# First three weight panels of each layer: own buffers, converted in the stage in front, the third panel in two token halves

## The chip, the cores and the metric

The kernel runs on one core of a Trainium2 chip. The metric is the device time of one execution in microseconds (us), and lower is better. Engines are named as in the profile: PE is TensorE (PEld its weight loads), ACT is ScalarE, DVE is VectorE, POOL is GpSimd, SP is SyncE, which issues the DMAs.

## What is computed

One sequence of 512 tokens with 1024 features (float32) goes through one block of a first kind and two layers of a second kind. The first block is a token mixer (convolution and an RWKV recurrence), then a feed-forward part (FFN):

```python
h = h + _rms_norm(mix, post_mix_g[l])
ffn = _channel_mixer(_rms_norm(h, pre_ffn_g[l]), ...)   # w_up 1024x5632, conv, gelu*up, w_down 2816x1024
h = h + _rms_norm(ffn, post_ffn_g[l])
```

Each layer of the second kind, run twice, is:

```python
h = _rms(x, norm_g[l])
proj = h @ w_in[l]
... = jnp.split(proj, SPLIT_AT, axis=-1)      # gq gk gv ga gz bq bk bv iq ik iw bz cq ck cv cz gate
y_a, y_b, y_c = gated linear attention, top-k attention, differential attention
merged = g0 * (y_a @ w_br[l, 0]) + g1 * (y_b @ w_br[l, 1]) + g2 * (y_c @ w_br[l, 2])
x = x + merged @ w_out[l]
```

## The kernel before

Five engines run five instruction streams written out by hand; semaphores that count each engine's finished steps order them. There are four stages: `mixer`, `ffn`, `layer` 0 and `layer` 1 (in `program`).

**Split products.** Every large product is made of three matmuls on float32r parts: weight hi x h hi, weight hi x h lo, weight lo x h hi (`project`, PE line L596). The weights come in panels, mostly 1024 rows x 256 columns, held as 128 x 2048. A panel goes through four steps. SP loads it into `m.raw` ("w raw"), ACT copies it to `m.wh` (`split_hi`, L352), DVE subtracts to get `m.wl` (`split_lo`, L393), and PE uses both ("w used"). `split_hi_halves` and `split_lo_halves` (L364, L374) do the two steps in halves. The three tensors have two slots each, taken in turn by the panel's running number `g`. So SP loads panel p when "w lo" of p-2 is done, and ACT converts it when PE has used p-2.

**The entry of a layer.** The stage in front ends with partial sums for blocks of 128 tokens. In the FFN these are the last two down panels, kk = 9 and 10 (`down`, L2036), in the order (9,0), (9,1), (10,0), (10,1), (9,2), (9,3), (10,2), transposes of blocks 0 and 1, (10,3). In layer 0 they are the last two `out` panels in a like order. Between the stages lies a seam. For each block of tokens: ACT sums squares (`post_sum`, `pre_sum`: L418, L421), DVE scales and adds (`post_add`: L466, L470, L474; `half_add`: L482) and norms (`pre_norm`: L490, L496, the result is xn), PE transposes (`seam_turn`, L586), ACT copies to h_hi (`seam_hi`, L447), DVE makes h_lo (`seam_lo`, L457). Blocks 0 and 1 come first, then 2 and 3.

The layer's first panels are iq[0] (256 columns), `lows` (ik, ga and iw together, 88 columns, three DMAs) and iq[1] (256 columns), then gk. In `tensor`, iq[0] and lows run first for tokens 0 to 255 (half 0), then for tokens 256 to 511 (half 1) with the transposes of blocks 2 and 3 between; iq[1] runs after both, over all 512 tokens. In `scalar` and `vector` the conversions of panels 0 and 1 (`high(0)`, `high(1)`, `low(0)`, `low(1)`) stand between the steps of the seam, the halves of panel 2 behind them.

**SP's order.** In the FFN the load of down panel kk waits for "w lo" of kk-2. Then come the layer's panels 0 and 1, each behind "w lo" of two panels before, then `rows_in` (14 small DMAs: 8 rows of norm gains, 4 lambda vectors, 2 of the gate projection), then panel 2 and the rest.

**ACT and DVE at the FFN's end.** For kk from 2 to 10 ACT does w_hi of down panel kk (not for 10), then the copy ffn_hi of kk (L2095), which waits for PE to have used kk-2; after the loop w_hi of panel 10 in halves. DVE does ffn_lo (L2142), then w_lo, and at the end w_lo of panel 10 in halves.

Of the kernel before, what the change touches and what calls it, by code (L numbers as in the profile page):

```python
# [12 lines left out]
F32 = mybir.dt.float32  # L13
# [5 lines left out]
P = 128  # L19
# [1925 lines left out]
def ffn(m, A, done, sems, seam, after, base):  # L1945
# [119 lines left out]
    def scalar(E):  # L2065
# [23 lines left out]
        for kk in range(2, DN):  # L2089
            if kk < DN - 1:  # L2090
                split_hi(E, m, down_base + kk, PANEL)
            E.wait_ge(act_done, E.so_far())
            E.wait_ge(dve_done, E.at(("G", 2 * kk + 1)))
            E.wait_ge(pe_done, E.at(("dn mm", kk - 2)))
            act.activation(m.gH[:, kk % 2, :, :], m.G[:, 2 * kk:2 * kk + 2, :], ACT.Copy).then_inc(act_done, 1)  # L2095
            E.counted(("g hi", kk))
        split_hi_halves(E, m, down_base + DN - 1, PANEL)
        seam_table(E, m, after)

    def vector(E):  # L2100
# [67 lines left out]
def lay_out_layers(nc, m):  # L2168
# [50 lines left out]
    m.wa2 = take("gla_wa2", [LOWS + LOWS // 3, 256])  # L2219
    m.later = m.bd  # L2220
    at[0], end = m.fcol_at, at[0]
    m.lcol = take("layer_cols", [P, 16])
# [10 lines left out]
def layer(m, A, out, done, sems, l, base, seam, after):  # L2233

    pe_done, act_done, dve_done, pool_done = (done[n] for n in ("pe", "act", "dve", "pool"))
    PS = m.PS
    w_loaded = sems("w_loaded0"), sems("w_loaded1")
    rows_loaded, small_loaded, gain_loaded, stored = (sems(n) for n in ("rows_loaded", "small_loaded", "gain_loaded", "stored"))

# [39 lines left out]
    def view(buf, p):  # L2279
        a = panels[p]  # L2280
        return buf[:, (base + p) % 2, 0:a.kt * a.w].rearrange("p (k n) -> p k n", k=a.kt)

    def size(p):
        return panels[p].kt * panels[p].w
# [51 lines left out]
    def sync(E):  # L2336
# [21 lines left out]
        for p in range(NP):  # L2358
            E.wait_ge(*E.point(("w lo", base + p - 2)))
            v, at, n = view(m.raw, p), 0, 0  # L2360
            pieces, kt, k0 = panels[p].pieces, panels[p].kt, panels[p].k0
            ks = kt if len(pieces) > 1 else kt // 2
            for name, c, w in pieces:
                for k in range(0, kt, ks):
                    if name in (0, 1, 2):
                        s = A["w_br_2"][l, name, P * k:P * (k + ks), c:c + w]
                    else:
                        s = A[name][l, P * (k0 + k):P * (k0 + k + ks), c:c + w]
                    sp.dma_start(v[:, k:k + ks, at:at + w],
                                 s.rearrange("(k q) n -> q k n", q=P)).then_inc(w_loaded[(base + p) % 2], 16)  # L2370
                    n += 1
                at += w
            E.moved(("w raw", base + p), f"w_loaded{(base + p) % 2}", n)
            if p == 1:
# [32 lines left out]
    def tensor(E, banks):  # L2407
# [7 lines left out]
        def panel(p, only=None, half=None):  # L2415
            a = panels[p]
            E.wait_ge(*E.point(("w lo", base + p)))
            H, W = view(m.wh, p), view(m.wl, p)
            ts = slice(0, T) if half is None else slice(PW * half, PW * half + PW)
# [25 lines left out]
        def tokens_part(p, t, k):  # L2445
            a = panels[p]
            H, W = view(m.wh, p), view(m.wl, p)
# [88 lines left out]
        for half in range(2):  # L2536
            for q in range(2):
                E.wait_ge(dve_done, E.at(seam.key("lo", 2 * half + q, 1)))
            if half:
                panel(iq[0], half=1)  # L2540
                panel(lows, half=1)
            elif seam.post is None:
                panel(iq[0], only=0, half=0)
                seam_turn(E, m, banks, seam, 2)
                panel(iq[0], only=1, half=0)
                seam_turn(E, m, banks, seam, 3)
                panel(lows, half=0)
            else:
# [3 lines left out]
                seam_turn(E, m, banks, seam, 3)  # L2552
        panel(iq[1])
        E.wait_ge(*E.point("rows"))
# [156 lines left out]
    def scalar(E):  # L2711
        act = E.eng

        def high(p):
            if p < NP:
                split_hi(E, m, base + p, size(p))

# [125 lines left out]
        if seam.post is not None:  # L2843
            for t in range(2):
                post_sum(E, m, seam, t)
            for t in range(2):
                pre_sum(E, m, seam, t)
            high(0)
# [4 lines left out]
            high(1)  # L2853
        else:
            pre_sum(E, m, seam, 0)
            pre_sum(E, m, seam, 1)
            seam_hi(E, m, seam, 0)
            high(0)
            seam_hi(E, m, seam, 1)
        for t in range(2, TT):  # L2860
            pre_sum(E, m, seam, t)
        if seam.post is None:
            high(1)
# [150 lines left out]
        merged_hi(KT - 1)  # L3014
        high(outs[2])
        high(outs[3])
        if after:
            seam_table(E, m, after)

    def vector(E):  # L3020
# [152 lines left out]
        if seam.post is not None:  # L3173
            for t in range(2):
                post_add(E, m, seam, t)
            for t in range(2):
                pre_norm(E, m, seam, t)
            low(0)
            seam_lo(E, m, seam, 0)
            seam_lo(E, m, seam, 1)  # L3180
            for t in range(2, TT):
                post_add(E, m, seam, t)
            low(1)
        else:
# [3 lines left out]
            seam_lo(E, m, seam, 0)  # L3188
            low(0)
# [5 lines left out]
        if seam.post is None:  # L3195
            low(1)
# [196 lines left out]
        low(outs[1])  # L3393
        low(outs[2])
        low(outs[3])
        for t in order(outs[1]):
# [99 lines left out]
```

## Time and profile before

| what | value |
|---|---|
| runs | 1939.05, 1939.12, 1939.25 us; median 1939.12 |
| profiled execution, its own time | 1943.69 us |
| its span in the trace | 1942.0 us, 30355 instructions |
| mean granted clock of PE | 0.995 |
| PE, PEld, DVE, ACT, POOL busy | 98%, 79%, 60%, 39%, 2% |
| entry of layer 0, entry of layer 1 | about 715 to 770, about 1322 to 1372 us |

The profile is of one execution, and times in its rows count from the start of its span. A row of the timeline has the start, the busy time, the engine, the line of the kernel, what is written and read, and in brackets how long the engine stood before it and who released it. A matmul's end is modelled, and successive matmuls overlap, so their rate is read from their starts.

### The profile page before, as it was taken

What the parts mean: (1) busy time and instruction counts of PE and PEld (TensorE: products, weight loads), DVE (VectorE), ACT (ScalarE), POOL (GpSimd) and SP (SyncE); (2) the same over time, 40 slices, a digit from 0 to 9 for tenths busy, and PEclk for the clock granted to TensorE, in tenths of its full rate; (3) what the DMA queues carried; (4) which work ended last, traced back from release to release, by engine and by line L of the source; (5) the groups of instructions that cost most, each with busy time, mean ns of one, the idle gap of its engine ahead of it and who ended that gap; (6) DMA issues with size and microseconds to landing.
All of it is one profiled execution on the core that took longest, in us unless ns stands there. A gap on an engine that the chain in (4) does not pass through costs nothing.

```text
span 1942.0 us, 30355 instructions
## 1 busy us (share of the span) xinstructions
PE 1901.2 (98%) x12689; PEld 1538.2 (79%) x12689; DVE 1158.0 (60%) x1714; ACT 749.6 (39%) x1082; POOL 32.1 (2%) x72
## 2 busy tenths in 40 slices
PE   7999999999999999999999999999999999999999
PEld 5677778888888888787777788888787777778887
DVE  5854554677675344456687855545446678764534
ACT  5623333422222344533444434334533445334421
POOL 3000000020000000000000000000000000000000
PEclk9999999999999999999999999999999999999999
DMA  4311113233333323222123222232322222222232
GB/s 151 95 55 46 36 35 114 62 109 92 104 88 107 109 76 109 65 88 83 48 71 104 87 66 76 76 130 66 100 75 78 85 66 76 87 87 66 66 109 87
DMA packets 166021, 161.65 MB, mean 83 GB/s; under 512 B 13877, under 2 KB 150363, under 8 KB 165883
## 3 DMA queue, kind: packets, MB, share of 16 engines
q1 hardware_dynamic: 165184, 158.99, 26.0%
q8 instruction: 99, 1.62, 0.4%
q10 hardware_dynamic: 698, 0.71, 0.1%
q14 instruction: 40, 0.32, 0.1%
HBM read 157.59 MB, written 2.10 MB: 82 GB/s over the span
## 4 chain that ended last, share of the span: by engine, by line
PE 77%; DVE 2%; ACT 1%; issue 0%; ACTq 0%; DVEq 0%
PE psum L596 63%; PE psum L2036 5%; PE psum L2531 2%; PE psum L2508 1%; PE psum L586 1%; PE psum L2488 1%; PE psum L2516 1%; DVE w_lo L393 1%; PE psum L523 1%; ACT w_hi L352 0%; PE psum L532 0%; PE psum L2612 0%; DVE h_lo L457 0%; DVE ffn_normed L470 0%; PE psum L2597 0%; DVE w_lo L374 0%
## 5 line engine op out<-in xcount | busy, mean ns | idle before, releaser
L596 PE MATMUL psum<-h_hi,w_hi 128*128 128x512 f32 (+1 forms) x1568 | 611.7, 390 | 10.7 <-DVE h_lo L457 6.1
L596 PE MATMUL psum<-h_lo,w_hi 128*128 128x512 f32 (+1 forms) x1568 | 595.5, 380 | 0.0
L596 PE MATMUL psum<-h_hi,w_lo 128*128 128x512 f32 (+1 forms) x1568 | 595.4, 380 | 0.0
L393 DVE TENSOR_TENSOR w_lo<-w_raw,w_hi 128x2048 fp32r<-128x2048 f32 (+2 forms) x143 | 299.4, 2094 | 284.1 <-ACT w_hi L352 281.6
L352 ACT ACTIVATE w_hi<-w_raw 128x2048 fp32r<-128x2048 f32 (+1 forms) x148 | 260.8, 1762 | 369.8 <-PE psum L596 299.1
L596 PEld LDWEIGHTS psum<-h_hi,w_hi 128*128 128x128 f32 x1568 | 295.3, 188 | 88.1 <-issue 15.7
L596 PEld LDWEIGHTS psum<-h_hi,w_lo 128*128 128x128 f32 x1568 | 295.5, 188 | 56.3
L596 PEld LDWEIGHTS psum<-h_lo,w_hi 128*128 128x128 f32 x1568 | 295.7, 189 | 51.9 <-issue 0.2
L596 PE MATMUL psum<-w_hi,h_hi 128*128 128x512 f32 (+1 forms) x512 | 183.9, 359 | 2.6 <-DVE w_lo L393 1.7
L596 PE MATMUL psum<-w_lo,h_hi 128*128 128x512 f32 (+1 forms) x512 | 179.8, 351 | 0.0
L596 PE MATMUL psum<-w_hi,h_lo 128*128 128x512 f32 (+1 forms) x512 | 179.7, 351 | 0.0
L596 PEld LDWEIGHTS psum<-w_hi,h_hi 128*128 128x128 f32 x512 | 97.6, 191 | 30.0 <-issue 11.0
L596 PEld LDWEIGHTS psum<-w_hi,h_lo 128*128 128x128 f32 x512 | 97.7, 191 | 12.9
L596 PEld LDWEIGHTS psum<-w_lo,h_hi 128*128 128x128 f32 x512 | 97.7, 191 | 11.9 <-issue 0.2
L596 PE MATMUL psum<-y_hi,w_hi 128*128 128x512 f32 x192 | 80.1, 417 | 0.0
L596 PE MATMUL psum<-y_hi,w_lo 128*128 128x512 f32 x192 | 75.2, 392 | 0.0
L596 PE MATMUL psum<-y_lo,w_hi 128*128 128x512 f32 x192 | 75.1, 391 | 0.0
L2126 DVE TENSOR_SCALAR ffn_conv<-psum,ffn_cols 128x512 f32<-128x512 f32 x44 | 35.6, 810 | 63.3 <-PE psum L596 62.2
L2814 ACT ACTIVATE squares<-psum 128x512 f32<-128x512 f32 x48 | 28.7, 598 | 110.6 <-PE psum L596 110.2
L2036 PE MATMUL psum<-w_hi,ffn_hi 128*128 128x512 f32 x176 | 68.7, 390 | 0.5 <-DVE ffn_conv L2132 0.5
L2036 PE MATMUL psum<-w_lo,ffn_hi 128*128 128x512 f32 x176 | 68.5, 389 | 0.0
L2036 PE MATMUL psum<-w_hi,ffn_lo 128*128 128x512 f32 x176 | 68.5, 389 | 0.0
(370 smaller groups left out, 2185.5 us busy)
## 6 DMA issues: line engine op xcount, KB each, us to landing
w_raw<-in_w_in_dram SPq DMA_DIRECT2D x170, 512.0 KB, 4.4
w_raw<-in_w_up_dram SPq DMA_DIRECT2D x44, 512.0 KB, 5.1
w_raw<-in_w_out_dram SPq DMA_DIRECT2D x24, 512.0 KB, 4.5
w_raw<-in_w_br_dram SPq DMA_DIRECT2D x48, 256.0 KB, 3.0
w_raw<-in_w_down_dram SPq DMA_DIRECT2D x22, 512.0 KB, 4.3
x_first<-in_x_dram SPq DMA_DIRECT2D x4, 512.0 KB, 5.1
x_tokens<-in_x_dram SPq DMA_DIRECT2D x4, 512.0 KB, 5.1
out_dram<-x_tokens SPq DMA_DIRECT2D x4, 512.0 KB, 2.6
```

What stands on the lines that cost most here:

```text
L352: act.eng.activation(m.wh[:, g % 2, 0:n], m.raw[:, g % 2, 0:n], ACT.Copy).then_inc(act.done, 1)
L393: eng.eng.tensor_tensor(m.wl[:, g % 2, 0:n], m.raw[:, g % 2, 0:n], m.wh[:, g % 2, 0:n].bitcast(F32), ALU.subtract).then_inc(eng.done, 1)
L523: last = pe.eng.matmul(out[q, :], m.ind[:, kind, q], x[:, j, :], start=begin, stop=end, skip_group_check=True)
L586: last = pe.eng.transpose(m.PS[0:n, bank, rows * i:rows * i + rows], b, m.ident[at:at + rows, at:at + rows])
L596: last = pe.eng.matmul(out, a(k), b(k), start=(opens and k == 0 and i == 0), stop=(k == kt - 1 and i == 2), skip_group_check=ks is not None)
L2036: last = pe.matmul(PS[:, 2 * t + n, :], g[:, kk % 2, k, tt], w[:, k, cc], start=(kk == 0 and k == 0 and i == 0), stop=(kk == DN - 1 and k ...
L2126: dve.tensor_scalar(c, z, tap[2], bias, ALU.mult, ALU.add).then_inc(dve_done, 1)
L2488: pe.matmul(o[:, 0:vis], m.Q[r, h // 2, P * i:P * i + P], m.ikf[r, 0:vis], start=True, stop=True).then_inc(pe_done, 1)
L2508: last = pe.matmul(o[:, 0:vis], m.Q[r, h, P * i:P * i + P], m.K[r, h, 0:vis], start=True, stop=True)
L2516: pe.matmul(o[:, 0:vis], m.Q[:, h, P * i:P * i + P], m.K[:, h, 0:vis], start=True, stop=True).then_inc(pe_done, 1)
L2531: last = pe.matmul(o[:, 0:P], m.V[:, k, P * h:P * h + P], m.PT[:, u % 2, P * k:P * k + P], start=(k == 0), stop=(k == i))
L2814: act.activation(m.sq3[:, 2 * (r % 2) + i, :], PS[:, bank(p, i), :], ACT.Tanh, scale=0.5).then_inc(act_done, 1)
```

## The change

Panels 0, 1 and 2 of each layer no longer use the two slots. Each has its own raw and hi buffer, laid over parts of the layers' arena that are free at that time; its lo is written over its raw. SP loads them without a wait for a slot: for layer 0 after the FFN's last "G", for layer 1 after "dsa lo" of layer 0. Their order to the other DMAs stays, `rows_in` between panels 1 and 2. Panels 3 and 4 take the slots behind the last two panels of the stage in front (`slot_user`).

In the FFN, ACT converts panels 0, 2, 1 after ffn_hi of kk = 9, and DVE subtracts in the same order after w_lo of kk = 9. In layer 0, ACT converts panels 0 and 1 between w_hi of the third and of the fourth `out` panel and panel 2 after the fourth; DVE subtracts 0 and 1 before the w_lo of the fourth, and panel 2 inside the seam, after h_lo of block 0. The conversions in the entries go. ACT's `high(3)` and DVE's `low(3)` follow the seam, `high(4)` and `low(4)` come where `step(iq[1])` had them or sooner.

iq[1] runs in two token halves, its first behind the transposes of blocks 2 and 3, its second last, and uses PSUM banks 3 and 5 instead of 0 and 1.

```diff
+def spare_hi(act, first, g, i):
+    raw, hi, _ = first[i]
+    act.wait_ge(*act.point(("w raw", g + i)))
+    act.wait_ge(act.done, act.so_far())
+    act.eng.activation(hi[:, :], raw[:, :], ACT.Copy).then_inc(act.done, 1)
+    act.counted(("w hi", g + i))
+
+def spare_lo(dve, first, g, i):
+    raw, hi, lo = first[i]
+    dve.wait_ge(dve.done, dve.so_far())
+    dve.wait_ge(dve.sems["act"], dve.at(("w hi", g + i)))
+    dve.eng.tensor_tensor(lo[:, :], raw[:, :], hi[:, :].bitcast(F32), ALU.subtract).then_inc(dve.done, 1)
+    dve.counted(("w lo", g + i))
@@ ffn, scalar: after "g hi" of kk
+            if kk == DN - 2:
+                E.wait_ge(dve_done, E.at(("g lo", 7)))
+                for i in (0, 2, 1):
+                    spare_hi(E, m.first, down_base + DN, i)
@@ ffn, vector: after w_lo of kk
+            if kk == DN - 2:
+                for i in (0, 2, 1):
+                    spare_lo(E, m.first, down_base + DN, i)
@@ lay_out_layers
+    spare = o - 4 * KB + 3 * 4 * PANEL
+    m.first = []
+    for i, n, lo_at, hi_at in ((0, PANEL, o - 4 * KB, q + 8 * KB), (1, KT * LOWP, spare, spare + 4 * KT * LOWP),
+                               (2, PANEL, o - 4 * KB + 8 * PANEL, o - 4 * KB + 4 * PANEL)):
+        m.first.append((take(f"first_raw{i}", [P, n], F32, over=lo_at), take(f"spare_hi{i}", [P, n], F32R, over=hi_at),
+                        take(f"spare_lo{i}", [P, n], F32R, over=lo_at)))
@@ layer
+    def slot_user(p):
+        return base + p - {3: 4, 4: 6}.get(p, 2)
@@ layer, bank
+        if p == iq[1]:
+            return 3 + 2 * i
@@ layer, sync
         for p in range(NP):
-            E.wait_ge(*E.point(("w lo", base + p - 2)))
+            if p == 0 and l == 0:
+                E.wait_ge(dve_done, E.before(None, ("G", FT - 1)))
+            if p == 0 and l:
+                E.wait_ge(dve_done, E.before(l - 1, ("dsa lo", NH - 1)))
+            if p >= 3:
+                E.wait_ge(*E.point(("w lo", slot_user(p))))
@@ layer, tensor
             if half:
                 panel(iq[0], half=1)
                 panel(lows, half=1)
+                panel(iq[1], half=1)
             elif seam.post is None:
                 panel(iq[0], only=0, half=0)
                 seam_turn(E, m, banks, seam, 2)
                 panel(iq[0], only=1, half=0)
+                panel(lows, half=0)
                 seam_turn(E, m, banks, seam, 3)
-                panel(lows, half=0)
+                panel(iq[1], half=0)
             else:
                 panel(iq[0], half=0)
                 panel(lows, half=0)
                 seam_turn(E, m, banks, seam, 2)
                 seam_turn(E, m, banks, seam, 3)
-        panel(iq[1])
+                panel(iq[1], half=0)
@@ layer, scalar: entry (high(0) and high(1) go from both branches)
         seam_hi(E, m, seam, 2)
         seam_hi(E, m, seam, 3)
+        high(3)
         evac(iq[0], 0)
-        split_hi_halves(E, m, base + 2, size(2))
         evac(iq[0], 1)
+        high(4)
         evac(lows, 0)
-        high(3)
-        step(iq[1])
+        evac(iq[1], 0)
+        evac(iq[1], 1)
@@ layer, scalar: end
         high(outs[2])
+        if after:
+            spare_hi(E, m.first, base + NP, 0)
+            spare_hi(E, m.first, base + NP, 1)
         high(outs[3])
         if after:
+            spare_hi(E, m.first, base + NP, 2)
             seam_table(E, m, after)
@@ layer, vector: entry (low(0) and low(1) go from both branches)
             seam_lo(E, m, seam, 0)
-            low(0)
+            spare_lo(E, m.first, base, 2)
             half_add(E, m, seam, 2)
...
-        split_lo_halves(E, m, base + 2, size(2))
         low(3)
-        step(iq[1])
+        low(4)
@@ layer, vector: end
         low(outs[2])
+        if after:
+            spare_lo(E, m.first, base + NP, 0)
+            spare_lo(E, m.first, base + NP, 1)
         low(outs[3])
```

## Rows read from the trace of the kernel before

**Rows 1.** The page: busy time, share of the span and instructions

```profile
PE 1901.2 (98%) x12689; PEld 1538.2 (79%) x12689; DVE 1158.0 (60%) x1714; ACT 749.6 (39%) x1082; POOL 32.1 (2%) x72
```

**Rows 2.** Waits of PE, 693 to 772 (waited for: us, times, longest)

```profile
PE psum L596 <- DVE h_lo L457: 3.2, 2, 2.5
PE psum L596 <- DVE w_lo L374: 1.0, 1, 1.0
PE psum L596 <- DVE w_lo L393: 0.4, 1, 0.4
```

**Rows 3.** Timeline of PE, 1337 to 1359: start, us, engine, line, operation [idle before <-releaser]

```profile
1338.31 0.36 PE L596 MATMUL psum<-h_hi,w_hi 128*128 128x256 f32 x1 [0.42 <-DVE h_lo L457]
...
1358.39 0.50 PE L596 MATMUL psum<-h_hi,w_hi 128*128 128x512 f32 x1 [0.98 <-DVE w_lo L374]
```

**Rows 4.** Timeline of PE, 731 to 746

```profile
731.57 0.28 PE L596 MATMUL psum<-h_lo,w_hi 128*128 128x256 f32 x1
...
737.08 0.28 PE L596 MATMUL psum<-h_hi,w_lo 128*128 128x256 f32 x1
...
745.07 0.36 PE L596 MATMUL psum<-h_hi,w_hi 128*128 128x256 f32 x1 [2.50 <-DVE h_lo L457]
```

**Rows 5.** Windows of PE: length, busy (x), granted clock, DMA share, GB/s

```profile
746.34:749.72 3.38, 3.38 (x18) 0.50 0.00 0
364.00:371.00 7.00, 5.13 (x30) 0.76 0.47 129
375.00:380.00 5.00, 2.50 (x22) 1.00 0.01 3
```

**Rows 6.** Timeline of DVE, 700 to 740

```profile
708.41 1.23 DVE L2142 TENSOR_TENSOR ffn_lo<-ffn_hidden,ffn_hi 128x1024 fp32r<-128x1024 f32 x1 [5.38 <-ACT ffn_hi L2095]
...
709.67 2.48 DVE L374 TENSOR_TENSOR w_lo<-w_raw,w_hi 128x1024 fp32r<-128x1024 f32 x2
...
726.03 2.29 DVE L393 TENSOR_TENSOR w_lo<-w_raw,w_hi 128x2048 fp32r<-128x2048 f32 x1 [0.52 <-ACT w_hi L352]
...
734.24 1.28 DVE L470 SCALAR_TENSOR_TENSOR ffn_normed<-psum,row_stats,post_ffn_gain 128x1024 f32<-128x1024 f32 x1
...
736.82 0.89 DVE L393 TENSOR_TENSOR w_lo<-w_raw,w_hi 128x704 fp32r<-128x704 f32 x1
...
737.94 1.28 DVE L496 SCALAR_TENSOR_TENSOR x_tile<-x_tokens,row_stats,layer_gain 128x1024 f32<-128x1024 f32 x1
```

**Rows 7.** Timeline of ACT, 705 to 735

```profile
707.25 1.06 ACT L2095 ACTIVATE ffn_hi<-ffn_hidden 128x1024 fp32r<-128x1024 f32 x1 [7.87 <-PE psum L2036]
...
708.40 2.16 ACT L364 ACTIVATE w_hi<-w_raw 128x1024 fp32r<-128x1024 f32 x2
...
732.32 0.79 ACT L352 ACTIVATE w_hi<-w_raw 128x704 fp32r<-128x704 f32 x1
```

**Rows 8.** Chain that ended last, 705 to 775: start, us, what

```profile
756.33 11.20 PE psum L596 x48
```

**Rows 9.** Timeline of DVE, 1325 to 1340

```profile
1333.70 2.29 DVE L393 TENSOR_TENSOR w_lo<-w_raw,w_hi 128x2048 fp32r<-128x2048 f32 x1 [2.04 <-ACT w_hi L352]
```

**Rows 10.** Timeline of ACT, 1300 to 1320

```profile
1314.45 1.92 ACT L352 ACTIVATE w_hi<-w_raw 128x2048 fp32r<-128x2048 f32 x1 [8.96 <-PE psum L596]
```

**Rows 11.** Timeline of SP's DMA queue, 690 to 720

```profile
692.18 0.80 SPq L1976 DMA_DIRECT2D w_raw<-in_w_down_dram  x2
...
703.06 10.96 SPq L2369 DMA_DIRECT2D w_raw<-in_w_in_dram  x5
...
719.26 0.28 SPq L2355 DMA_DIRECT2D gla_wa<-in_gla_ba_dram  x1
```

**Rows 12.** DMA issues, 690 to 710 and 1300 to 1330: count, KB, us to landing

```profile
w_raw<-in_w_in_dram SPq DMA_DIRECT2D x2, 512.0 KB, 4.1
...
layer_gain<-in_norm_g_dram SPq DMA_DIRECT2D x1, 512.0 KB, 6.7
```

**Rows 13.** Timeline of PE at the last down panel

```profile
712.41 0.40 PE L2036 MATMUL psum<-w_hi,ffn_hi 128*128 128x512 f32 x1
```

More of the change, by code:

```diff
@@ L2161 @@
 LOWS = RANK + IH
+LOWP = 64 + LOWS
 TAU = 16.0
@@ L2220, in lay_out_layers @@
     m.later = m.bd
+    spare = o - 4 * KB + 3 * 4 * PANEL
[4 more added lines that the diff above has]
+                        take(f"spare_lo{i}", [P, n], F32R, over=lo_at)))
+    assert spare + 8 * KT * LOWP <= pt + 2 * KB
     at[0], end = m.fcol_at, at[0]
@@ L2237, in layer @@
     w_loaded = sems("w_loaded0"), sems("w_loaded1")
+    first_loaded = [sems(f"first_loaded{i}") for i in range(3)]
     rows_loaded, small_loaded, gain_loaded, stored = (sems(n) for n in ("rows_loaded", "small_loaded", "gain_loaded", "stored"))
@@ L2281, in view, with hi_view, lo_view @@
         return buf[:, (base + p) % 2, 0:a.kt * a.w].rearrange("p (k n) -> p k n", k=a.kt)
+    def hi_view(p):
+        return m.first[p][1][:, :].rearrange("p (k n) -> p k n", k=KT) if p < 3 else view(m.wh, p)
+    def lo_view(p):
+        return m.first[p][2][:, :].rearrange("p (k n) -> p k n", k=KT) if p < 3 else view(m.wl, p)
+    def slot_user(p):
+        return base + p - {3: 4, 4: 6}.get(p, 2)
     def size(p):
@@ L2358, in sync @@
         for p in range(NP):
-            E.wait_ge(*E.point(("w lo", base + p - 2)))
-            v, at, n = view(m.raw, p), 0, 0
+            if p == 0 and l == 0:
[4 more added lines that the diff above has]
+                E.wait_ge(*E.point(("w lo", slot_user(p))))
+            v, at, n = view(m.raw, p), 0, 0
+            name = f"w_loaded{(base + p) % 2}"
+            loaded = w_loaded[(base + p) % 2]
+            if p < 3:
+                v = m.first[p][0][:, :].rearrange("p (k n) -> p k n", k=KT)
+                name, loaded = f"first_loaded{p}", first_loaded[p]
             pieces, kt, k0 = panels[p].pieces, panels[p].kt, panels[p].k0
             ks = kt if len(pieces) > 1 else kt // 2
-            for name, c, w in pieces:
+            for src, c, w in pieces:
                 for k in range(0, kt, ks):
-                    if name in (0, 1, 2):
-                        s = A["w_br_2"][l, name, P * k:P * (k + ks), c:c + w]
+                    if src in (0, 1, 2):
+                        s = A["w_br_2"][l, src, P * k:P * (k + ks), c:c + w]
                     else:
-                        s = A[name][l, P * (k0 + k):P * (k0 + k + ks), c:c + w]
+                        s = A[src][l, P * (k0 + k):P * (k0 + k + ks), c:c + w]
                     sp.dma_start(v[:, k:k + ks, at:at + w],
-                                 s.rearrange("(k q) n -> q k n", q=P)).then_inc(w_loaded[(base + p) % 2], 16)
+                                 s.rearrange("(k q) n -> q k n", q=P)).then_inc(loaded, 16)
                     n += 1
                 at += w
-            E.moved(("w raw", base + p), f"w_loaded{(base + p) % 2}", n)
+            E.moved(("w raw", base + p), name, n)
             if p == 1:
@@ L2417, in panel @@
             E.wait_ge(*E.point(("w lo", base + p)))
-            H, W = view(m.wh, p), view(m.wl, p)
+            H, W = hi_view(p), lo_view(p)
             ts = slice(0, T) if half is None else slice(PW * half, PW * half + PW)
@@ L2446, in tokens_part @@
             a = panels[p]
-            H, W = view(m.wh, p), view(m.wl, p)
+            H, W = hi_view(p), lo_view(p)
             tt = slice(P * t, P * t + P)
@@ L2715, in high @@
             if p < NP:
-                split_hi(E, m, base + p, size(p))
+                E.wait_ge(*E.point(("w raw", base + p)))
+                E.wait_ge(act_done, E.so_far())
+                E.wait_ge(pe_done, E.at(("w used", slot_user(p))))
+                act.activation(m.wh[:, (base + p) % 2, 0:size(p)], m.raw[:, (base + p) % 2, 0:size(p)],
+                               ACT.Copy).then_inc(act_done, 1)
+                E.counted(("w hi", base + p))
         def evac(p, i):
@@ L2847, in scalar @@
                 pre_sum(E, m, seam, t)
-            high(0)
             seam_hi(E, m, seam, 0)
@@ L2852, in scalar @@
                 post_sum(E, m, seam, t)
-            high(1)
         else:
@@ L2857, in scalar @@
             seam_hi(E, m, seam, 0)
-            high(0)
             seam_hi(E, m, seam, 1)
@@ L2861, in scalar @@
             pre_sum(E, m, seam, t)
-        if seam.post is None:
-            high(1)
         seam_hi(E, m, seam, 2)
         seam_hi(E, m, seam, 3)
+        high(3)
         evac(iq[0], 0)
-        split_hi_halves(E, m, base + 2, size(2))
         evac(iq[0], 1)
+        high(4)
         evac(lows, 0)
-        high(3)
-        step(iq[1])
+        evac(iq[1], 0)
+        evac(iq[1], 1)
         E.wait_ge(act_done, E.so_far())
@@ L3182, in vector @@
                 post_add(E, m, seam, t)
-            low(1)
         else:
@@ L3188, in vector @@
             seam_lo(E, m, seam, 0)
-            low(0)
+            spare_lo(E, m.first, base, 2)
             half_add(E, m, seam, 2)
@@ L3194, in vector @@
             pre_norm(E, m, seam, t)
-        if seam.post is None:
-            low(1)
         seam_lo(E, m, seam, 2)
         seam_lo(E, m, seam, 3)
-        split_lo_halves(E, m, base + 2, size(2))
         low(3)
-        step(iq[1])
+        low(4)
         E.wait_ge(dve_done, E.so_far())
```

## The prediction

> **What bounds the kernel now.** The page's busy line comes first: TensorE (PE) works 98% of the span [rows 1], so time can come only from the few places where it waits, or from its clock. The table of what PE waited for, cut to the stretch in which the first layer begins, shows the most of them: there it waits 3.2 us for h_lo, 1.0 us for the halved w_lo of the third panel and 0.4 us for the second panel's w_lo [rows 2]. At the second layer's entry the timeline has two waits, 0.42 and 0.98 us [rows 3], and at the first one it shows the longest single one, 2.5 us before 745.07 [rows 4]. The windows view shows a loss that no wait row lists: from 746.34 to 749.72, just behind that gap, the granted clock is 0.50, the 1.2 GHz level, for 3.38 us [rows 5].
>
> A gap costs more than its wait row. A 128x256 matmul is drawn 0.28 us long, but from 731.57 to 737.08 lie 46 intervals, 0.12 us each [rows 4]. The drawn tail hides 0.16 us of each gap.
>
> **Part 1: what the entries can give.** First entry: 4.6 us of waits in four gaps, plus 4 x 0.16, is 5.2 us. The half clock goes with its gap: 16 matmuls of 256 columns at 0.213 us (256 columns at 1.2 GHz) instead of 0.12, 1.5 us. Where does each wait go, and what is late next?
> - VectorE (DVE) no longer does the first panel's w_lo at 726.03 (2.29 us) in front of the four h_lo pieces [rows 6]. It can follow ScalarE's h_hi pieces at once, so the last h_lo ends at about 730.3 instead of 731.2, no later than the down projection's last matmul. The 0.7 us gap closes.
> - The second panel's w_lo (0.89 us [rows 6]) and w_hi (0.79 us [rows 7]) are done before, so that gap closes too.
> - The 2.5 us gap is the chain transpose, h_hi, h_lo for tokens 256 to 511 with nothing for PE to do. The third panel's first half, 48 matmuls of 0.12 us or 5.8 us, now stands there, and the chain needs about 3. Its second tile uses bank 5, which h_lo of block 2 frees: with PE at the transposes at 739.1 that is about 742, and the tile starts at 743.9. Late next would be the transposes, which need xn 2. DVE gets there by two post adds from 730.8 (2.8 us each: from 734.24 to 737.94 less the 0.89 of the w_lo between) and one norm of 1.4 us, 737.8 [rows 6]: 1.3 us ahead of PE.
> - The 1.0 us gap closes because the third panel is ready before the stage.
>
> Price: the third panel ran 48 matmuls of 512 columns in 11.2 us [rows 8]. In halves it is 96 x 0.12 = 11.5 us, 0.35 us worse. The Trainium skill ("TensorE: Matmul & The Clock Gate", section "Wait — 56ns, not 53.3ns?") gives a matmul at full clock its columns over 2.4 GHz plus about 2.5 ns. By it the halving would cost 48 x 2.5 ns, 0.12 us; the rows have the dearer price.
>
> First entry: 5.2 + 1.5 - 0.35 = 6.4 us. Second entry: 1.4 + 2 x 0.16 - 0.35 = 1.4 us. There DVE stood 2.04 us until ScalarE's w_hi and then worked 2.29 us on w_lo at 1333.70 [rows 9]; the third panel's w_lo now goes in without that stand, ends at about 1334.0, and h_lo is no longer behind PE. **Entries together: 7.8 us.**
>
> **Part 2: what the moved work costs where it now stands.** In layer 0 it is free: ScalarE idles 8.96 us before its w_hi at 1314.45 [rows 10], and 1.92 + 0.79 us go in there; the third panel's 1.92 us stand behind it, before the sums of the entry. Without that cover the last out panel's w_lo would be late, which is about 1 us ahead of its use.
>
> In the FFN it is not free. Follow the queues.
> - SyncE (SP): the last down load goes out at 692.18 (0.80 us for two) [rows 11]. Panels 0 to 2 now wait for nothing, so panel 0 goes out at 693.0, 0.9 us for its two DMAs. Panel 1's three take 1.9 us: from the end of the last down w_lo, 709.67 + 2.48 = 712.15 [rows 6], to the end of the group at 703.06 + 10.96 = 714.02 [rows 11]. The 14 small row loads behind them take from there to 719.26 + 0.28, 5.5 us [rows 11]. So panel 2 goes out only at 693.0 + 0.9 + 1.9 + 5.5 = 701.3. A 512 KB load lands 4.1 us after its issue [rows 12], the second at 701.8 + 4.1 = **705.9**.
> - ScalarE converts panel 0 before that, then stands on panel 2's raw: 705.9 + 1.92 = 707.9, and panel 1 to 708.7. Behind them in order is the last ffn_hi (1.06 us), which started at 707.25 [rows 7]: now 708.7 to 709.8, then the two w_hi halves (2.16 us [rows 7]) to 712.0.
> - DVE: panel 2's w_lo 707.95 to 710.2, panel 1's 0.89 us to 711.15, ffn_lo 1.23 us to 712.4, the halves 2.48 us to 714.9 [rows 6].
> - PE takes the last down panel at 712.41 [rows 13] and could have from 712.15, 0.26 us in hand. Now it can from 714.9 and starts at about 715.0: a **new stall of 2.6 us**. All of the entry behind it hangs on the sums that PE then makes, so it goes through whole. If panel 2 landed before 701.3, DVE's own work would still end at about 712.3: no stall to speak of. With 6.7 us, the slowest 512 KB load in these rows [rows 12], it is 5.2 us. I take 4.1, the row for the same tensor into an idle queue.
>
> The clock: the windows at 364 and 746.34 hold or follow gaps of 1.9 and 2.5 us and have a low clock (0.76, 0.50); that at 375 has 2.50 us of PE work missing and 1.00 [rows 5]. So the new stall probably brings some 3.4 us at half clock, 1.7 us lost; the bounds are 0 and, by the same length once more, 3.4. The same page of the skill ("What's actually happening" and what follows) says that the chip's watch on activity runs free of the kernel, so that one gap may fall well or badly. The row at 375 agrees.
>
> **Sum:** -7.8 + 2.6 + 1.7 = -3.5 us. The profiled execution took 1943.69 us around its span of 1942.0; the median is 1939.12, 4.6 us less. I carry the difference over: 1939.1 - 3.5 = **1935.6 us**.
>
> **Rivals.**
> - *Stall without a low clock*, as at 375: -7.8 + 2.6 = -5.2, 1933.9 us. Chance 0.20.
> - *No stall*, panel 2 landing early enough: 1931.3 us. The 5.5 us of row loads speak against it. Chance 0.12.
> - *Longer stall*, the load taking 6.7 us: -7.8 + 5.2 + 1.7 = -0.9, 1938.2 us. Chance 0.09.
> - *Slower*: the same wait of ScalarE for panel 2's raw in front of the last ffn_hi. Each microsecond of lateness is one of stall; slower by 0.2% needs a stall of 7.8 + 3.9 - 1.7 = 10.0 us, so a landing at 713.3 or later, as if the small row loads held the queue 7.4 us after their issue: from 1943.0 us. Nobody waited for them before, so no row excludes it; the DMA share shows none of it. Chance 0.04.
> - *The change doesn't do what it says*: the entries keep half their waits, since xn 2 or bank 5 is later than worked out here: -3.9 + 4.3 = +0.4, 1939.5 us. Chance 0.05.
>
> **Chances and range.** A measurement of this kernel tells about 0.2%, 3.9 us, from no change. The likeliest case (0.50) lies at -3.5, just inside; with the landing 0.5 us earlier it is -4.0, so a third of it counts as faster. Faster: 0.16 + 0.20 + 0.12 = 0.48. Slower: 0.04, and 0.01 of the last rival. The same: the rest, 0.47. The likeliest case alone is 1934.8 to 1936.4. The range reaches down to the case without a stall and up most of the way to the longer one: 1931.2 to 1937.4.
>
> **What would show it.** Right: in the list of PE's waits a new one of 2 to 3 us for the halved w_lo near 712; ScalarE idle from about 701 to 706, ended by a DMA, before the third panel's w_hi; a window of clock 0.50 near 716; no PE wait over 0.2 us at either entry; from the last down matmul to the first gk matmul 6.4 us less. Wrong: no wait at 712; a wait of PE for xn or for bank 5; a matmul interval other than 0.12 us in the third panel.

## The result and the profile after

| | before | after |
|---|---|---|
| median of 18 runs each, us | 1939.31 (1937.49 to 1943.30) | 1945.32 (1942.35 to 1950.49) |
| ratio | | 1.0028, 95% interval 1.0021 to 1.0036 |
| profiled execution, own time and span, us | 1943.69, 1942.0 | 1947.30, 1945.5 |

The change made the kernel slower by 0.28%, 5 to 6 us. The forecast was 3.5 us faster, with a range up to 1937.4. So the sign is wrong.

From the page of the changed kernel, its first part (busy time of the engines, share of the span, instructions) and, behind the dots, the shares of the engines in the chain that ended last:

```profile
PE 1900.0 (98%) x12785; PEld 1540.7 (79%) x12785; DVE 1157.2 (59%) x1712; ACT 749.2 (39%) x1080; POOL 32.1 (2%) x72
...
PE 76%; SPq 1%; DVE 1%; ACT 1%; DMA 1%; issue 0%; ACTq 0%; DVEq 0%
```

TensorE (PE) is as busy as before [rows 1], but SyncE's queue (SPq) and DMA now stand in the chain with 1% each. The waits of PE say where (us in total, times, longest). In the changed kernel, FFN's end and first entry, 693 to 790:

```profile
PE psum L2054 <- DVE w_lo L374: 7.4, 1, 7.4
```

The same view of the second entry, 1300 to 1400:

```profile
PE psum L604 <- DVE x_tile L514: 1.8, 1, 1.8
PE psum L614 <- DVE w_lo L393: 0.4, 1, 0.4
```

The four waits of [rows 2] are gone, and the two of [rows 3] too. In their place stands one wait of 7.4 us for the halved w_lo, in front of the last down panel. At the second entry there is a new one of 1.8 us for the normed block (x_tile, the xn of the prediction), and before it, at 1322.2, one of 0.4 us for a w_lo of layer 0. The timeline of ScalarE (ACT) at the FFN's end, changed kernel (start, duration in us, what; in brackets the idle time before it and what ended that):

```profile
696.69 1.06 ACT L2113 ACTIVATE ffn_hi<-ffn_hidden 128x1024 fp32r<-128x1024 f32 x1
698.84 1.92 ACT L403 ACTIVATE spare_hi<-first_raw 128x2048 fp32r<-128x2048 f32 x1 [1.09 <-DMA first_raw<-in_w_in_dram]
709.20 2.80 ACT L403 ACTIVATE spare_hi<-first_raw 128x2048 fp32r<-128x2048 f32 x2 [8.44 <-DMA first_raw<-in_w_in_dram]
712.03 1.06 ACT L2113 ACTIVATE ffn_hi<-ffn_hidden 128x1024 fp32r<-128x1024 f32 x1
713.17 2.15 ACT L364 ACTIVATE w_hi<-w_raw 128x1024 fp32r<-128x1024 f32 x2
```

The timeline of VectorE (DVE) there:

```profile
711.21 3.22 DVE L412 TENSOR_TENSOR spare_lo<-first_raw,spare_hi 128x2048 fp32r<-128x2048 f32 x2 [7.49 <-ACT spare_hi L403]
714.47 1.22 DVE L2164 TENSOR_TENSOR ffn_lo<-ffn_hidden,ffn_hi 128x1024 fp32r<-128x1024 f32 x1
715.73 2.48 DVE L374 TENSOR_TENSOR w_lo<-w_raw,w_hi 128x1024 fp32r<-128x1024 f32 x2
```

To be compared with [rows 7] and [rows 6]. ACT stands 8.44 us on a DMA, panel 2's raw, which is there at 709.20. The last ffn_hi is queued behind it, and ffn_lo and the halves of w_lo on DVE behind that, to 718.2. The order is the one the prediction follows, step by step; only the time of the landing differs. Why it landed late, the chain of the changed kernel between 685 and 790 shows (start, us, what; SPq is SyncE issuing):

```profile
692.43 0.66 SPq L2424
...
693.13 2.73 SPq L2424
...
695.90 2.59 SPq L2424
...
698.54 0.58 SPq L2393
...
703.96 0.39 SPq L2424
...
704.40 4.78 DMA first_raw<-in_w_in_dram
...
718.36 16.24 PE psum L2054 x60
...
771.83 11.70 PE psum L614 x96
```

Panel 1's three DMAs held SP from 692.43 to 698.49, 6.1 us, where the kernel before needed 1.9 [rows 11, with rows 6]. Then came the 14 small row loads, 5.4 us (5.5 before), then panel 2, whose second DMA took 4.8 us from the start of its issue to its landing. Windows of PE show the clock around it (stretch; its length, PE busy with instructions, granted clock, DMA share, GB/s):

```profile
713.40:723.70 10.30, 5.34 (x13) 0.51 0.44 140
718.40:723.70 5.30, 5.30 (x13) 0.52 0.86 272
```

PE idles from 710.9, the clock falls to half (1.2 GHz) at 713.4 while PE is still idle, and stays there until 723.7. The last 5.3 us of it lie under work. The timeline of PE, in that stretch and behind it:

```profile
722.33 0.63 PE L2054 MATMUL psum<-w_hi,ffn_hi 128*128 128x512 f32 x1
722.76 0.63 PE L2054 MATMUL psum<-w_hi,ffn_lo 128*128 128x512 f32 x1
...
724.23 0.39 PE L2054 MATMUL psum<-w_hi,ffn_hi 128*128 128x512 f32 x1
724.45 0.39 PE L2054 MATMUL psum<-w_hi,ffn_lo 128*128 128x512 f32 x1
```

Twelve matmuls of 512 columns start 0.43 us apart, where at the full clock they start 0.23 us apart: 12 x 0.20 = 2.4 us lost. This spell is three times as long as the one at 746 in [rows 5], but half of it lies under the stall and costs nothing more.

**The account, profile against profile.** PE's marks are the start of the last down panel and of the first gk panel of each layer. The chain of the kernel before has the two gk panels:

```profile
769.76 11.70 PE psum L596 x96
...
1371.79 11.70 PE psum L596 x96
```

In the changed kernel they are at 771.83 and 1375.33. The timeline of ACT of the kernel before has the ffn_hi of kk = 9:

```profile
698.32 1.06 ACT L2095 ACTIVATE ffn_hi<-ffn_hidden 128x1024 fp32r<-128x1024 f32 x1
```

PE came to the last down panel at 712.41 before [rows 13] and, since that ffn_hi is 1.63 us earlier after (696.69), at 710.8 there. That difference stems from the part in front, which the change does not touch: there PE's clock is at half in both profiles for a few short spells, at other times in each (before: near 150, 302 to 309 and 368, some 6.9 us lost by the granted clock; after: near 301, 366 and 376, some 5.2). From there to gk: 57.35 us before, 61.05 after, +3.7. From gk to gk: 602.03 and 603.50, +1.5. From the second gk to the end: 570.2 in both. So +5.2 us belong to the change, and -1.6 is chance in front of it; the 18 runs, which average over such chance, say +6.0 by the medians and +5.4 by the ratio.

### The profile page after: what moved, and what is told of

Same layout as the page of the kernel before. It is cut to its first block, busy times and chain, and to the rows that moved or that the text cites. A ratio compares the mean times of both kernels' runs of the same rounds, so it can differ in the third digit from the quotient of the medians.

```text
span 1945.5 us, 30538 instructions
## 1 busy us (share of the span) xinstructions
PE 1900.0 (98%) x12785; PEld 1540.7 (79%) x12785; DVE 1157.2 (59%) x1712; ACT 749.2 (39%) x1080; POOL 32.1 (2%) x72
## 4 chain that ended last, share of the span: by engine, by line
PE 76%; SPq 1%; DVE 1%; ACT 1%; DMA 1%; issue 0%; ACTq 0%; DVEq 0%
PE psum L614 63%; PE psum L2054 5%; PE psum L2586 2%; PE psum L604 1%; PE psum L2563 1%; PE psum L2543 1%; PE psum L2571 1%; SPq L2424 1%; PE psum L541 1%; DMA first_raw<-in_w_in_dram 1%; DVE w_lo L393 0%; PE psum L550 0%; PE psum L2669 0%; SPq L2393 0%; PE psum L2654 0%
## 5 line engine op out<-in xcount | busy, mean ns | idle before, releaser
L614 PE MATMUL psum<-h_hi,w_hi 128*128 128x512 f32 (+1 forms) x1440 | 571.1, 397 | 4.7 <-DVE h_lo L475 2.5
L614 PE MATMUL psum<-h_hi,w_lo 128*128 128x512 f32 (+1 forms) x1440 | 555.7, 386 | 0.0
L614 PE MATMUL psum<-h_lo,w_hi 128*128 128x512 f32 (+1 forms) x1440 | 555.6, 386 | 0.0
L393 DVE TENSOR_TENSOR w_lo<-w_raw,w_hi 128x2048 fp32r<-128x2048 f32 (+1 forms) x139 | 293.0, 2108 | 279.2 <-ACT w_hi L2776 263.3
L614 PEld LDWEIGHTS psum<-h_hi,w_hi 128*128 128x128 f32 x1440 | 272.0, 189 | 79.2 <-issue 16.0
L614 PEld LDWEIGHTS psum<-h_hi,w_lo 128*128 128x128 f32 x1440 | 271.9, 189 | 54.8
L614 PEld LDWEIGHTS psum<-h_lo,w_hi 128*128 128x128 f32 x1440 | 272.2, 189 | 50.8 <-issue 0.2
L2776 ACT ACTIVATE w_hi<-w_raw 128x2048 fp32r<-128x2048 f32 (+1 forms) x98 | 167.2, 1706 | 241.7 <-PE psum L614 237.1
L352 ACT ACTIVATE w_hi<-w_raw 128x2048 fp32r<-128x2048 f32 x46 | 88.2, 1917 | 114.9 <-PE psum L2054 64.8
L614 PE MATMUL psum<-y_lo,w_hi 128*128 128x512 f32 x192 | 75.1, 391 | 0.0
L2054 PE MATMUL psum<-w_hi,ffn_lo 128*128 128x512 f32 x176 | 69.4, 395 | 0.0
```

The lines of the kernel that those rows point to most:

```text
L352: act.eng.activation(m.wh[:, g % 2, 0:n], m.raw[:, g % 2, 0:n], ACT.Copy).then_inc(act.done, 1)
L614: last = pe.eng.matmul(out, a(k), b(k), start=(opens and k == 0 and i == 0), stop=(k == kt - 1 and i == 2), skip_group_check=ks is not None)
L2054: last = pe.matmul(PS[:, 2 * t + n, :], g[:, kk % 2, k, tt], w[:, k, cc], start=(kk == 0 and k == 0 and i == 0), stop=(kk == DN - 1 and k ...
L2776: act.activation(m.wh[:, (base + p) % 2, 0:size(p)], m.raw[:, (base + p) % 2, 0:size(p)], ACT.Copy).then_inc(act_done, 1)
```

## The experiments

Theory A: PE lost time since ACT stands in order on panel 2's raw, which is late because SP is late to issue it. Within it, A2 says that panel 1's three DMAs issue slowly because loads ahead of them are still in flight, A3 that they cost 6 us into the new buffers whatever is in flight. Rivals: the added conversions themselves fill ACT and DVE (B); the small rows are to blame (C); the token halves cost more than worked out (D). Nine kernels were run, called versions 1 to 9, each beside the kernel before on the same chip, which took 1939.5 to 1941.0 us there, so ratios are compared. Each is the changed kernel with the edit shown.

**1. Row loads behind panel 2.**

```diff
-            if p == 1:
+            if p == 2:
                 if l:
                     E.wait_ge(pe_done, E.before(l - 1, ("spv", NU - 1)))
                 rows_in()
```

> Changed kernel with the 14 small row loads issued behind panel 2 instead of in front of it. Theory A (ScalarE stands on panel 2's raw, which is late because SyncE is late to issue it; panel 1's three DMAs take 6.1 us to issue there instead of 1.9): the load goes out 5.4 us earlier, so the stall of TensorE in front of the last down panel goes from 7.4 to about 2 us, and its 1.8 us wait for x_tile at the second entry goes; about 1937.5 us, 8 less than the changed kernel's 1945.3. Rival B (the added conversions themselves fill ScalarE and VectorE): the stall stays at 7.4 us, 1945 us.

Measured 1937.96 us, ratio 0.9984 (0.9975 to 0.9993). Its waits of PE at the FFN's end:

```profile
PE psum L2054 <- DVE w_lo L374: 2.6, 1, 2.6
```

Its timeline of ACT there:

```profile
702.14 2.81 ACT L403 ACTIVATE spare_hi<-first_raw 128x2048 fp32r<-128x2048 f32 x2 [3.62 <-DMA first_raw<-in_w_in_dram]
```

Panel 2's raw is there at 702.14. Counted from the ffn_hi in front (694.47 here, 696.69 in the changed kernel), it lands 4.8 us earlier, and the stall is 4.8 us shorter, 2.6 us. The wait for x_tile at the second entry is gone. Versions 7 and 8 give the same: the landing 2.1 us later and 1.8 us earlier, the stall 2.1 longer and 1.8 shorter. Each microsecond of the landing is one of stall. B is out as the cause of the long stall. The window of PE behind the stall, version 1:

```profile
711.40:714.90 3.50, 3.50 (x9) 0.56 0.73 214
```

Here the half clock ends at 714.5, 3.2 us after PE resumed, and it costs 3.5 x (1 - 0.56) = 1.5 us.

**2. Panel 2 in front of panel 1.**

```diff
-        for p in range(NP):
+        for p in (0, 2, 1, *range(3, NP)):
```

> Changed kernel with SyncE's order panel 0, panel 2, panel 1, small rows. Theory A: panel 2's raw lands about 698, before ScalarE needs it, and panel 1's slow issue stands behind it; the stall of TensorE in the FFN is under 1 us, no wait for x_tile at the second entry, about 1933 us. If only the small rows were to blame (rival C), this one would be no better than the version that moves them alone. Rival B: stall unchanged, 1945 us.

Measured 1939.57 us, ratio 0.9993 (0.9984 to 1.0002), not the 1933 expected. PE waits once in both stretches, at the end of layer 0 (waits of PE, version 2):

```profile
PE psum L614 <- DVE w_lo L393: 3.2, 1, 3.2
```

The timeline of ACT there:

```profile
1303.71 1.92 ACT L403 ACTIVATE spare_hi<-first_raw 128x2048 fp32r<-128x2048 f32 x1 [7.43 <-DMA first_raw<-in_w_in_dram]
1308.53 0.79 ACT L403 ACTIVATE spare_hi<-first_raw 128x704 fp32r<-128x704 f32 x1 [2.90 <-DMA first_raw<-in_w_in_dram]
1309.41 1.92 ACT L2776 ACTIVATE w_hi<-w_raw 128x2048 fp32r<-128x2048 f32 x1
```

The FFN's stall is gone, as expected. But now panel 1 is the late load, and in layer 0 ACT converts it in front of the last out panel: it stands 2.90 us on the DMA, and w_hi at 1309.41 comes late. That is the same mechanism in the place where the prediction saw about 1 us in hand. C is half right: with the first version it shows that the small rows lie in the way of panel 2, but their 5.5 us were in the sum; what was not in it is the length of panel 1's issue.

**3. SP as it is, but nothing on PE's path behind the load.**

```diff
@@ ffn, scalar (vector has the same with spare_lo, split_lo_halves)
             if kk == DN - 2:
                 E.wait_ge(dve_done, E.at(("g lo", 7)))
-                for i in (0, 2, 1):
-                    spare_hi(E, m.first, down_base + DN, i)
+                spare_hi(E, m.first, down_base + DN, 0)
         split_hi_halves(E, m, down_base + DN - 1, PANEL)
+        spare_hi(E, m.first, down_base + DN, 2)
+        spare_hi(E, m.first, down_base + DN, 1)
```

> Changed kernel with SyncE as it is, but in the FFN ScalarE and VectorE convert panels 2 and 1 behind the last down panel's halves instead of in front. Theory A: the load stays late (lands about 709) but nobody on TensorE's path stands behind it: no stall in front of the last down panel, the wait for x_tile at the second entry stays (1.8 us), about 1935 us. Rival B: the same work in the same two engines only moves the wait to the sums of the entry, a wait of some 3 us there, 1942 us or more.

Measured 1935.18 us, ratio 0.9972 (0.9962 to 0.9982). Its timeline of ACT at the FFN's end:

```profile
703.08 1.06 ACT L2113 ACTIVATE ffn_hi<-ffn_hidden 128x1024 fp32r<-128x1024 f32 x1 [4.94 <-PE psum L2054]
...
706.85 2.81 ACT L403 ACTIVATE spare_hi<-first_raw 128x2048 fp32r<-128x2048 f32 x2 [0.46 <-DMA first_raw<-in_w_in_dram]
```

Its waits of PE at the second entry:

```profile
PE psum L604 <- DVE x_tile L514: 1.2, 1, 1.2
PE psum L614 <- DVE w_lo L393: 0.5, 1, 0.5
```

PE does not wait at all between 690 and 800. The load is as late as before (12.7 us behind ffn_hi of kk = 9, which started at 694.17; 12.5 in the changed kernel), and ACT waits 0.46 us for it behind its due work. The second entry keeps its waits. The ratio is that of the sum with no stall in the FFN and the loss at the second entry left in (see the table behind version 9).

**4. Without the token halves.** TensorE's order is put back; the buffers stay.

```diff
             if half:
                 panel(iq[0], half=1)
                 panel(lows, half=1)
-                panel(iq[1], half=1)
...
-                panel(iq[1], half=0)
+        panel(iq[1])
```

> Changed kernel without the token halves of the third panel (TensorE's order as before the change; the separate buffers stay). The halves are worth, by the sum on record, the 2.5 us gap at the first entry with its tail and perhaps 1.5 us of half clock, less 0.35 us for each layer: 2 to 3.5 us slower than the changed kernel, 1947.5 to 1949 us, with the stall of 7.4 us unchanged. If the halves themselves were the loss (rival D), it would be faster than 1945 us.

Measured 1949.25 us, ratio 1.0047 (1.0035 to 1.0060), 3.7 us above the changed kernel by the ratios, where 2 to 3.5 were expected. D is out. The first entry has its old wait again, as the waits of PE in version 4 show, 690 to 800:

```profile
PE psum L2054 <- DVE w_lo L374: 7.8, 1, 7.8
PE psum L614 <- DVE h_lo L475: 2.5, 1, 2.5
```

Behind this 2.5 us gap, which ends at 752.00, the granted clock is 1.00 (window 745 to 765), where the same gap in the kernel before was followed by 3.4 us at half clock [rows 5].

**5. Both entries mended, with SP's rows moved.** Edits 1 and 3, and at the end of layer 0:

```diff
             spare_hi(E, m.first, base + NP, 0)
-            spare_hi(E, m.first, base + NP, 1)
         high(outs[3])
         if after:
             spare_hi(E, m.first, base + NP, 2)
+            spare_hi(E, m.first, base + NP, 1)
@@ vector: spare_lo of panel 1 goes behind that of panel 2, in the second entry
```

> Changed kernel with three edits: in the FFN panels 2 and 1 are converted behind the last down panel's halves; the small row loads are issued behind panel 2; at the end of layer 0 the last out panel's w_hi and w_lo come before those of panel 1. Theory A: nothing on TensorE's path stands behind a load any more, so no wait over 0.3 us at either entry or in front of the last down panel, and the whole 7.8 us of the first part of the sum show: 0.9960 of the kernel before, about 1931.5 us where that takes 1939.3. If the entries give less than the sum says, the ratio stays near the 0.9972 of the version with the first edit alone.

Measured 1933.10 us, ratio 0.9966 (0.9954 to 0.9978). No wait of PE in either stretch. From gk to gk: 1360.27 less 759.78, 600.5 us, 1.5 less than before (1.4 in the sum). The ratio expected lies in the interval.

**6. Both entries mended, SP untouched.** Edit 3, and panel 2 converted in the second entry:

```diff
@@ layer, scalar, entry without post norm
             pre_sum(E, m, seam, 0)
+            spare_hi(E, m.first, base, 2)
             pre_sum(E, m, seam, 1)
@@ end of layer 0: high(outs[3]), then spare_hi of panel 1; vector as in 5
```

> Changed kernel with SyncE's order untouched (panel 2's raw as late as in the changed kernel, about 5 us later than with the row loads behind it). In the FFN panels 2 and 1 are converted behind the last down panel; in layer 0 panel 1 is converted behind the last out panel, panel 2 in the second entry behind the first sum of squares. Theory A (what costs is who stands behind the load, not the lateness): as fast as the version with SyncE's order mended, 0.9960, with no wait for x_tile. If lateness itself costs, 0.9972 or worse with a wait for w_lo of panel 2.

Measured 1930.90 us, ratio 0.9953 (0.9941 to 0.9966), the fastest of all, 9.1 us below the kernel before by the ratio. PE waits nowhere in the two stretches. The timeline of ACT in version 6, second entry:

```profile
1301.44 1.92 ACT L403 ACTIVATE spare_hi<-first_raw 128x2048 fp32r<-128x2048 f32 x1 [7.21 <-DMA first_raw<-in_w_in_dram]
1303.44 1.92 ACT L2778 ACTIVATE w_hi<-w_raw 128x2048 fp32r<-128x2048 f32 x1
...
1312.07 1.06 ACT L436 ACTIVATE layer_squares<-x_tokens 128x1024 f32<-128x1024 f32 x1 [4.31 <-DVE x_tokens L500]
...
1313.64 1.92 ACT L403 ACTIVATE spare_hi<-first_raw 128x2048 fp32r<-128x2048 f32 x1
```

Here the late load cost PE nothing, since what was due on ACT stood in front of its conversion. The intervals of versions 5 and 6 overlap, so which is better is not settled.

**7. SP waits for panel 0's landing before it issues panel 1.**

```diff
+            if p == 1:
+                E.wait_ge(*E.point(("w raw", base)))
```

> Changed kernel in which SyncE waits for panel 0 to have landed before it issues panel 1. Theory A2 (panel 1's three DMAs, 3072 small rows, issue slowly since the queue is still full of the 2 MB in front of them): with an empty queue their issue takes 1.9 us as in the kernel before instead of 6.1, panel 2 goes out within 1.5 us of where it did, and the time stays at 1945 to 1946 us. Rival A3 (those DMAs cost 6 us to issue into the new buffers, whatever is in the queue): issue 6 us again, panel 2's raw another 6 us later, stall 13 us, about 1952 us.

Measured 1946.95 us, ratio 1.0035 (1.0023 to 1.0047). Its chain has panel 1's three DMAs (start, us):

```profile
695.85 0.37 SPq L2426
...
696.26 0.58 SPq L2426
...
696.88 1.05 SPq L2426
```

They take 2.1 us from 695.85 to 697.93. The same three instructions into the same buffer took 6.1 us in the changed kernel. What was different is what SP's queue still had in flight. Rival A3 is out. The wait itself cost more than was expected: panel 2 went out 1.8 us later than in the changed kernel, counted from the ffn_hi in front, and not within 1.5; the stall was 9.5 us, and the time lies 1 us above the 1945 to 1946 expected.

**8. Panel 1 in front of panel 0.** The loop runs over `(1, 0, *range(2, NP))`, and the rows follow panel 0.

> Changed kernel with SyncE's order panel 1, panel 0, small rows, panel 2: the same DMAs and bytes ahead of panel 2, but panel 1's three slow ones have 1 MB in flight in front of them instead of 2. Theory A2 (their issue waits for what is in flight): about 3.5 us instead of 6.1 for the three, panel 2's raw some 2.5 us earlier, the stall in front of the last down panel about 5 us instead of 7.4; ratio to the kernel before about 1.0010 to 1.0020. If only the count of DMAs and bytes ahead of panel 2 counts, and not what is in flight at panel 1's issue, the stall stays at 7.4 us and the ratio at 1.0028.

Measured 1944.55 us, ratio 1.0020 (1.0010 to 1.0030), stall 5.6 us. The three DMAs in its chain:

```profile
688.33 0.43 SPq L2424
...
688.80 0.58 SPq L2424
...
689.43 2.85 SPq L2424
```

4.0 us with one panel (the last down load, 1 MB) in flight, against 2.1 with none and 6.1 with two; 3.5 us were expected. The landing moved with it, 1.8 us instead of 2.5. Part of the gain was lost again at the end of layer 0, where PE waited 2.5 us for a w_lo.

**9. The second entry alone.** Layer 0's end and the second entry as in 6, the FFN as changed.

> Changed kernel with the FFN as it is and only layer 0's end and the second entry edited: panel 1 converted behind the last out panel, panel 2 in the second entry behind the first sum of squares. Theory A: the wait of 1.8 us for x_tile and the 0.4 us for w_lo go, the 7.4 us stall stays: 2.2 us less than the changed kernel, ratio to the kernel before 1.0017 instead of 1.0028.

Measured 1942.01 us, ratio 1.0011 (1.0003 to 1.0020): 0.0017 below the changed kernel, 3.3 us, more than the 2.2 expected, though the intervals (1.0021 to 1.0036 and this one) are each as wide as that difference. PE has no wait at the second entry; the stall in the FFN is 7.7 us. The 2.2 counted only PE's two waits; the way from gk to gk is 3.1 us shorter than in the changed kernel.

**All profiles side by side.** Three stretches of each profile, in us: from the ffn_hi of kk = 9 to the first gk panel, from gk to gk, from there to the end. Behind them, what the first two differ from before, and what the ratio of the runs says, with half the width of its interval.

| kernel | to gk | gk to gk | to the end | by profile | by ratio |
|---|---|---|---|---|---|
| before | 71.4 | 602.0 | 570.2 | | |
| changed | 75.1 | 603.5 | 570.2 | +5.2 | +5.4 (1.5) |
| 1, rows behind panel 2 | 69.4 | 601.1 | 570.2 | -2.9 | -3.1 (1.7) |
| 2, panel 2 in front | 65.3 | 604.0 | 570.2 | -4.2 | -1.4 (1.7) |
| 3, FFN's order | 65.1 | 603.1 | 570.1 | -5.3 | -5.4 (1.9) |
| 4, no halves | 77.8 | 603.2 | 570.1 | +7.6 | +9.1 (2.4) |
| 5, both entries, SP moved | 65.1 | 600.5 | 570.1 | -7.9 | -6.6 (2.3) |
| 6, both entries | 65.1 | 600.4 | 570.2 | -7.9 | -9.1 (2.4) |
| 7, SP waits | 76.3 | 604.8 | 570.1 | +7.6 | +6.8 (2.3) |
| 8, panel 1 first | 72.6 | 603.3 | 570.3 | +2.4 | +3.9 (1.9) |
| 9, second entry alone | 75.3 | 600.4 | 570.2 | +2.2 | +2.1 (1.6) |

With no stall the way to gk is 65.1 us in three versions, 6.3 less than before. Only version 2 stands outside its interval: its 11 runs go from 1935.57 us at a mean clock of 1.000 to 1941.87 at 0.995, and the profiled one, 1936.55, is among its fastest. Why so many of them had the lower clock is not shown.

## Why the prediction was wrong

**What bounds, and what the entries give: right.** All six gaps closed, and none of the rivals for them (xn 2 or bank 5 late at the first entry) came. First entry: 57.35 us before; from the start of the last down panel at 718.36 to gk at 771.83 it is 53.47, of which 2.4 are half clock, so 51.1: 6.3 us gained against 6.4 in the sum, as in the table. Second entry: 1.5 against 1.4 in version 5. The half clock at 746 is gone with its gap. That its 1.5 us are in both the sum and the measurement is in part luck: version 4 has the gap without it. The halves cost a little less than was put down: 168 matmuls of half width follow on each other in 19.89 us in the changed kernel's chain:

```profile
749.71 19.89 PE psum L614 x168
```

That is 0.118 us each, 11.4 us for 96 of them, 0.2 more than the 11.2 of [rows 8], where the sum has 0.35 (its own numbers give 0.32).

**The stall: right place, right queue, wrong size.** The step that failed is "Panel 1's three take 1.9 us" in the list of SP. That duration was read where SP had stood on the last down w_lo and nothing was in flight [rows 11]. Moved up, the same DMAs stand behind 2 MB and took 6.1 us. With that, panel 2's issue is 4.2 us later. The landing took 4.8 us instead of 4.1. Most of that was a reading: 4.1 is the middle of the two DMAs in [rows 12], and the slower of the two took 4.6 there. Together 4.9 us, and 2.6 + 4.9 = 7.5 is the 7.6 us measured from 710.8 to 718.4. The rival "longer stall" had the right direction but looked for the lateness in the landing, and not in the issue. The slower one had ACT's wait right, but put the lateness on the small rows, which took 5.4 us, 0.1 less than in the sum. It asked for a landing 7.4 us late, and the actual 4.9 was enough together with the next two points.

**The clock: right that it falls, 1.7 us put down, 2.4 measured.** The upper bound of 3.4 held. In version 1, with a stall of 2.6 us as forecast, the spell costs 1.5; that case of the sum, -7.8 + 2.6 + 1.7 = -3.5, is 0.9982, and it measured 0.9984. Its landing is that of the forecast, 7.7 us behind the ffn_hi of kk = 9 (705.9 is 7.6 behind). So the sum stands once the landing is right.

**Layer 0's end: "free" was wrong.** This is the second step that failed, a term put at nothing: the prediction looked for room on ACT there ("ScalarE idles 8.96 us"), had panel 2's conversion right behind the w_hi that ends at 1316.4 [rows 10], and worked out no landing for it. The same slow issue brought its raw at 1325.87. SP's timeline in the changed kernel, its group of five DMAs:

```profile
1306.06 8.24 SPq L2424 DMA_DIRECT2D first_raw<-in_w_in_dram  x5
```

The last three of them, panel 1's, take 7.0 us, from 1307.28 to 1314.30, behind the last out panel, the gain and panel 0, 2.5 MB in all.

ACT's timeline there:

```profile
1314.59 2.86 ACT L403 ACTIVATE spare_hi<-first_raw 128x2048 fp32r<-128x2048 f32 x2 [7.06 <-DMA first_raw<-in_w_in_dram]
...
1325.87 1.92 ACT L403 ACTIVATE spare_hi<-first_raw 128x2048 fp32r<-128x2048 f32 x1 [6.42 <-DMA first_raw<-in_w_in_dram]
...
1329.40 1.06 ACT L436 ACTIVATE layer_squares<-x_tokens 128x1024 f32<-128x1024 f32 x1
```

And PE's:

```profile
1332.52 1.09 PE L604 MATMUL psum<-ident,x_tile 128*128 128x128 f32 x8 [1.84 <-DVE x_tile L514]
```

Behind it on ACT came the table load and the first sum of squares, so xn and PE's transposes were late by 1.84 us. The entry gave +1.5 instead of -1.4.

The account then is -6.3 + 7.6 + 2.4 + 1.5 = +5.2 us, against -6.4 + 2.6 + 1.7 - 1.4 = -3.5.

**Open.** What SP's issue waits for was not separated. Bytes ahead alone do not give it: 4.0, 6.1 and 7.0 us behind 1, 2 and 2.5 MB, but 6.2 us behind 3.5 MB at the end of layer 0 in version 2 (1297.33 to 1303.53). Where panel 0 is ahead, the third issue ends 0.2 to 0.4 us before ACT can take panel 0 (698.49 and 698.84 in the changed kernel, 1314.30 and 1314.59 at its layer 0's end, 1303.53 and 1303.71 in version 2), as if it waited for room that panel 0 frees; no run tests that.

Version 6's 9.1 us are 1.2 more than its profile says and 1.3 more than the sum, with an interval of 0.0013 to either side. The clock is where they may come from: the mean clock of its five runs is 0.999 to 1.000, that of the 17 runs of the kernel before beside it 0.995 to 0.999, and its profile has no spell at half clock within the span. In the part in front, which no version touches, its ffn_hi of kk = 9 starts at 693.47 and that of the kernel before at 698.32. Whether that is chance in five runs is not shown.

## What to carry to other kernels

The issue time of a DMA is not a constant of the instruction: that of three finely cut loads, read with an empty queue (1.9 us), was three times as long behind 2 MB (6.1 us), and all that SP issues behind it moves. Work out the landing of each moved load, also where its engine has room. When a conversion is moved to an earlier stage, ask what is queued behind it on its engine, and put the work that the bound engine waits for in front of any instruction that waits for a load; with that order alone the late load cost nothing (ratio 0.9953 instead of 1.0028). Check the same order in every stage that got the same edit: here version 2 cured the FFN and broke the end of layer 0.

## What the runs showed of the hardware that was not expected

- SP's issue of three DMAs (3 x 1024 rows of 256, 64 and 32 bytes) took 2.1 us with nothing in flight, 4.0 us behind 1 MB, 6.1 us behind 2 MB, 7.0 us behind 2.5 MB and 6.2 us behind 3.5 MB. The Trainium skill ("DMA: Bandwidth & Descriptors", section "Issuing engines are not separate DMA queues") calls the sequencer time to start DMAs "usually small relative to the DMA itself"; here that holds for the 512 KB loads (panel 0's two in the changed kernel 0.43 and 0.51 us, against 5.8 and 6.9 us to the landing); panel 1's second and third took 2.73 and 2.59 us to issue, against 7.4 and 4.9 us to the landing, and there the measurement decides.
- A stall of 7.4 us brought a half clock of 10.3 us, one of 2.6 us a spell that ended 3.2 us after the work resumed. A gap of 2.5 us was followed by 3.4 us of it in the kernel before and by none in version 4. The fall came during the long stall, and the return only 5.3 us after PE was busy again. The Trainium skill says that the watch runs free of the kernel ("TensorE: Matmul & The Clock Gate", "What's actually happening"); the two gaps of 2.5 us agree with it, and no run here tests it.
